# Two-tile router rows, and the third expert pair's weights loaded ahead of the first gather

## The chip, the core and the metric

The kernel runs on one core of one Trainium2 chip. The metric is the device time of one execution in microseconds; 2% decides a verdict, and the time before is the median of three runs.

## The reference

Two layers. Each has a token mixer (layer 0: RWKV-7, layer 1: stick-breaking attention), a 4-head cross-attention into 256 memory tokens, and a hierarchical mixture of experts (MoE). All are pre-RMSNorm with a residual add, on 512 tokens of 1024 channels in float32. The part that matters here:

```python
def _hierarchical_moe(h, wg, bg, we, be, w1, w3, w2):
    g_logits = (t @ wg) + bg                       # 4 groups
    group = jnp.argmax(g_logits, axis=-1)
    e_logits = ((t @ we) + be).reshape(-1, G, E)   # 8 experts in each group
    top_val, top_idx = lax.top_k(e_sel, TOP_K)     # two experts of the chosen group
    ...
    for gi in range(G):
        hid = silu(t @ w1) * (t @ w3)              # 1024 -> 256
        y = y + (hid * gate) @ w2                  # 256 -> 1024
```

## The kernel before, in words

All engines run hand-written queues and meet through semaphores. One big on-chip array (`arena`, cut into slots of 1024 columns by `at(slot, shape)`) and one more (`ring`) hold everything but the residual `h`.

In a layer the output projection of cross-attention (`xo0`, `xo1`, TensorE line L656) completes the residual tile by tile (4 tiles of 128 tokens), and the router runs between its groups. For each tile ScalarE (`moe_route_act`) squares the rows (L2317), scales and writes out the transposed tile that TensorE made (L562, into `xTE`), takes the root (L2323), scales the rows (L2306, into `tnE`) and stores them in DRAM (`normed_rows`, L2308). TensorE transposes (L552, through three banks, so the fourth transpose of a tile waits until ScalarE has written out the first), computes the logits (L2258) and ranks (L2275, L2276); VectorE chooses the experts. Then the MoE gathers rows from `normed_rows` by a table (GpSimd, L2601).

The 32 experts are worked as 16 pairs, n = 0 to 15. For a pair TensorE does the up matmuls (L2713), turns the hidden rows (L2728), turns the next pair's rows (L2698) and does the down matmuls of the pair before (L2738). A pair's weights are 4 pieces of up weights (`load_up`: w1 and w3 of two experts, L2544 and L2545) and 2 pieces of down weights (`load_down`, L2548), each 1 MB. Two buffer sets alternate, and pair 2's up weights have a place of their own (`w13x`, slots 12 to 20). SyncE issues all of these loads in one fixed order, and each waits until the pair before it in its buffer is done:

- `moe_first_loads`: pair 0, during cross-attention.
- `moe_route_loads`: the router's own weights; `moe_loads`: pair 1, as the ring's slots come free.
- Then, when all rows are stored, all logits done and the first gather has landed (`xg_in0`): pair 2's up weights into `w13x`.
- Up of pair 4 (after pair 0's up matmuls), up of pair 3 (after pair 1's up), down of pair 2 (after pair 0's down), down of pair 3 (after pair 1's down), up of pair 5 (after pair 3's up), and so on.

Slots 12 to 20 are `tnE` (4 tiles of rows, slots 12 to 16) and `xTE` (4 transposed tiles, slots 16 to 20) while the router runs, which is why pair 2's up weights wait for it. Slots 28 to 32 are the memory's keys and values, used in both layers.

Of the kernel before, what the change touches and what calls it, by code (L numbers as in the profile page):

```python
# [11 lines left out]
P = 128  # L12
C = 1024
T = 512
# [117 lines left out]
def trunk(nc, A, out, scratch):  # L132

    ctx = ExitStack()
    with ctx:
# [395 lines left out]
        def late_bank(name, n):  # L531

            return 5 + n % 3 if name[:3] == "ffn" else 4 + n % 4
# [20 lines left out]
        def late_evac(eng, name, t, dst, which, step=2):  # L554

            for k in range(which, KC, step):
                n = LATE0[name] + KC * t + k
                eng.wait_ge(S("late_turned"), n + 1)
                g = gainT[:, GAIN[name], k:k + 1]
                d, v = dst[:, k, P * t:P * t + P], PS[:, late_bank(name, n), 0:P]  # L560
                if which == 0 or step == 1:
                    eng.activation(d, v, ACT.Copy, scale=g).then_inc(S("late_act"), 1)  # L562
                else:
                    eng.tensor_scalar(d, v, g, None, ALU.mult).then_inc(S("late_vec"), 1)
# [1572 lines left out]
        def so_vec(vec):  # L2137
# [4 lines left out]


        NPE = NE // 2
        tnE = at(12, [NT, C])
        xTE = at(16, [KC, T])
        ringS = ring[:, :, :, :].rearrange("p r k n -> p (r k n)")


# [3 lines left out]
        w2e = [[split(arena[:, 6144 * a + 4096:6144 * a + 6144], [2, C]) for a in range(2)],  # L2153
               [split(ringS[:, 2048 * a:2048 * a + 2048], [2, C]) for a in range(2)]]
        w13x = [at(12 + 4 * a, [2, KC, F]) for a in range(2)]
        xg = [at(20 + p, [C]) for p in range(2)]
        xgT = [at(22 + p, [KC, P]) for p in range(2)]
        ye = [at(24 + p, [C]) for p in range(2)]
# [83 lines left out]

        def moe_route_loads(sp, l):

            sp.wait_ge(S("proj_filled"), FIRST[f"xo{l}"] + 1)
            sp.dma_start(wge[:, :, 0:G], A["moe_wg"][l].rearrange("(p k) n -> p k n", k=KC)).then_inc(S("route_in"), 16)
            sp.dma_start(wge[:, :, G:], A["moe_we"][l].rearrange("(p k) n -> p k n", k=KC)).then_inc(S("route_in"), 16)
            sp.dma_start(bge[:, 0:G], bcast(A["moe_bg"][l])).then_inc(S("route_in"), 16)
            sp.dma_start(bge[:, G:], bcast(A["moe_be"][l])).then_inc(S("route_in"), 16)

        def route_logits(pe, l, t):

            if t == 0:
                pe.wait_ge(S("route_in"), 64 * (l + 1))
            scores_read(pe, l, (0, 1, 3, 6)[t])
            for k in range(KC):
                tile_there(pe, f"ffn{l}", t, k)
                ins = pe.matmul(PS[:, 4, HD * t:HD * t + G + NE], xTE[:, k, P * t:P * t + P], wge[:, k, :],  # L2258
                                start=(k == 0), stop=(k == KC - 1))
            ins.then_inc(S("logits"), 1)  # L2260

# [39 lines left out]
        def moe_route_act(act, l):  # L2301
            name, ready = f"ffn{l}", h_tile_ready(f"xo{l}")

            def rows(t):
                act.wait_ge(S("ffn_rstd"), 5 * l + (1, 2, 4, 5)[t])
                act.activation(tnE[:, t, :], h[:, t, :], ACT.Copy, scale=rstd[:, t:t + 1]).then_inc(S("norm_rows"), 1)  # L2306
                act.wait_ge(S("norm_rows"), ROWS0[name] + t + 1)
                act.dma_start(scratch["rows"][P * t:P * t + P, :], tnE[:, t, :]).then_inc(S("rows_out"), 16)  # L2308

            act.activation(warm[:, :], gn_eps[:, :], ACT.Sqrt).then_inc(S("table_warm"), 1)  # L2310
            for t in range(NT):
                last = t == NT - 1
                ready(act, t)
                if last:
                    late_evac(act, name, t, xTE, 0, 1)
                end, total = 512 if last else C, sumsq[:, t:t + 1]
                act.activation(tnE[:, t, 0:end], h[:, t, 0:end], ACT.Square, accum_out=total).then_inc(S("ffn_norm"), 1)  # L2317
                if not last:
                    late_evac(act, name, t, xTE, 0, 1 if t else 2)
                act.wait_ge(S("ffn_norm"), 9 * l + (1, 3, 5, 8)[t])  # L2320
                if last:
                    act.wait_ge(S("ffn_rstd"), 5 * l + 3)
                act.activation(rms[:, t:t + 1], total, ACT.Sqrt, scale=1.0 / C,  # L2323
                               bias=half_mean[:, :] if last else ffn_eps[:, :]).then_inc(S("ffn_norm"), 1)
                if t and not last:
                    rows(t - 1)
                if t == NT - 2:
                    group_evacuated(act, FIRST[f"xo{l}"] + 12)
                    act.activation(tnE[:, NT - 1, 512:C], h[:, NT - 1, 512:C], ACT.Square, accum_out=half_sq[:, :])\
                        .then_inc(S("ffn_norm"), 1)  # L2330
                if t == NT - 2:
                    rows(t)
            rows(NT - 1)
            act.activation(warm[:, :], gn_eps[:, :], ACT.Exp).then_inc(S("table_warm"), 1)
            act.wait_ge(S("route_a"), 2 * l + 2)
            act.activation(gdiff, gdiff, ACT.Exp).then_inc(S("route_exp"), 1)
            act.activation(ed, ed, ACT.Exp).then_inc(S("route_exp"), 1)
# [223 lines left out]
        def moe_loads(sp, l):  # L2561


            assert UNITS.index(f"xo{l}") % RING == 2
            load_up(sp, l, 2, w13[1][0], S("w13_in1"))
            sp.wait_ge(S("proj_filled"), FIRST[f"xo{l}"] + 11)
            load_up(sp, l, 3, w13[1][1], S("w13_in1"))
            sp.wait_ge(S("proj_filled"), FIRST[f"xo{l}"] + 13)
            for a in range(2):
                load_down(sp, l, 2 + a, w2e[1][a], S("w2_in1"))  # L2570

            sp.wait_ge(S("rows_out"), 16 * NT * (l + 1))
            sp.wait_ge(S("logits"), NT * (l + 1))

            sp.wait_ge(S("xg_in0"), 16 * (NPE // 2 * l + 1))
            for a in range(2):
                load_up(sp, l, 4 + a, w13x[a], S("w13x_in"))

            def up_weights(n):
                sp.wait_ge(S("up_done"), NPE * l + (n - 3 if n == 4 else n - 1))  # L2580
                for a in range(2):
                    load_up(sp, l, 2 * n + a, w13[n % 2][a], S(f"w13_in{n % 2}"))

            def down_weights(n):

                sp.wait_ge(S("down_done"), NPE * l + n - 1)
                for a in range(2):
                    load_down(sp, l, 2 * n + a, w2e[n % 2][a], S(f"w2_in{n % 2}"))

            up_weights(4)  # L2590
            up_weights(3)
            down_weights(2)
            down_weights(3)
            for n in range(4, NPE):
                if n + 1 < NPE:
                    up_weights(n + 1)
                down_weights(n)
# [7 lines left out]
        def moe_pool(pool, l):  # L2605
# [6 lines left out]
            for p in range(2):  # L2612
                pool.memset(xg[p], 0.0).then_inc(S("xg_cleared"), 1)  # L2613
            pool.wait_ge(S("xg_cleared"), 2 * l + 2)
            pool.wait_ge(S("rows_out"), 16 * NT * (l + 1))
            pool.wait_ge(S("table_ready"), l + 1)
            for n in range(4):
                fetch(n)
# [112 lines left out]
        def hidT_out(act, rows):  # L2731
            return act.activation(hidT[:, :, 0:rows], bank(4, 4, P)[:, 0:2, 0:rows], ACT.Copy)

        def down(pe, p, n, half):
            for k in range(2):
                for a in range(n):
                    r = slice(BLK * a, BLK * a + BLK)
                    ins = pe.matmul(PS[r, 6 + half, :], hidT[:, k, r],  # L2738
                                    w2e[p][a][:, k, 512 * half:512 * half + 512], start=(k == 0), stop=(k == 1))
            return ins  # L2740

        def ye_free(eng, l, j, p):
# [11 lines left out]
        def moe_pe(pe, l):  # L2754
# [21 lines left out]
            def down_pair(n):  # L2776
                p = n % 2
                pe.wait_ge(S(f"w2_in{p}"), 32 * (NPE // 2 * l + n // 2 + 1))
                pe.wait_ge(S("hidT_ready"), NPE * l + n + 1)
                pe.wait_ge(S("ye_a"), NPE * l + n + l + 1)  # L2780
                down(pe, p, 2, 0).then_inc(S("down_half"), 1)
                pe.wait_ge(S("ye_v"), NPE * l + n + l + 1)
                down(pe, p, 2, 1).then_inc(S("down_done"), 1)

            pe.wait_ge(S("table_ready"), l + 1)
            for p in range(2):
# [131 lines left out]
        def further_pe(pe, l):  # L2918
# [6 lines left out]
            def body(j, at_step):  # L2925
                pe.wait_ge(S(f"over_gathered{l}"), 16 * (j + 1))
                step(at_step, 50)
                turn_rows(pe, 0, BLK).then_inc(st, 1)
                step(at_step, 52)
                up(pe, 0, 1, w13[0]).then_inc(st, 1)  # L2930
                step(at_step, 56)
                turn_hid(pe, BLK).then_inc(st, 1)
                step(at_step, 58)
                down(pe, 0, 1, 0)
                down(pe, 0, 1, 1).then_inc(st, 1)
                step(at_step, 61)
            further(pe, l, body)

# [203 lines left out]
```

## Time and profile before

| | |
|---|---|
| median of 3 runs | 1691.88 us (1688.39 to 1696.31) |
| profiled execution | 1693.46 us, span 1691.6 us |
| TensorE busy | 1527.1 us, 90% of the span |
| VectorE, ScalarE, GpSimd busy | 802.5, 418.7, 160.8 us |
| DMA | 315.04 MB, mean 186 GB/s |
| mean granted TensorE clock | 0.960 |

The span is from the first to the last instruction. The profile slices it in 40 parts; in the two MoE stretches (about 715 to 950 us and 1421 to 1650 us) the DMA engines are busy all the time, and moved 402 to 426 GB/s in a slice; in most slices between they are nearly idle. All times of day below are microseconds from the span's start.

### The profile page before, as it was taken

How to read it: one execution, taken by the hardware profiler on the slowest of the kernel's cores; microseconds unless marked ns; L12 is line 12 of the kernel's file. 1: busy time of each engine (PE TensorE's matmuls, PEld its weight loads, DVE VectorE, ACT ScalarE, POOL GpSimd, SP SyncE). 2: the span in 40 equal slices, each digit the busy share in tenths (PEclk: the TensorE clock that was granted, in tenths of full speed). 3: DMA queues.
4: the chain of work that ended last, by engine and by line, in shares of the span. 5: the costliest groups of instructions: out<-in, count | busy, mean ns of one | idle time of the engine just before them, and what ended most of it. 6: DMA issues, size and time to landing. Idle time of an engine off the chain costs nothing.

```text
span 1691.6 us, 28991 instructions
## 1 busy us (share of the span) xinstructions
PE 1527.1 (90%) x12509; PEld 943.0 (56%) x12509; DVE 802.5 (47%) x1403; ACT 418.7 (25%) x849; POOL 160.8 (10%) x183
## 2 busy tenths in 40 slices
PE   6999988989999999799788899999999997988777
PEld 4786777777645864534233388646468544333332
DVE  6655555653854355444121455546652544431225
ACT  2124255554201231301000120037321322100002
POOL 2000223230000000111110200000000001111101
PEclk9999999999999999799899999999999997989988
DMA  8208200011631412499999912220042116999995
GB/s 275 100 1 297 71 3 5 4 48 35 226 123 64 191 46 73 161 402 422 424 425 423 349 46 100 100 100 2 1 191 108 54 65 225 405 424 426 423 417 199
DMA packets 82338, 315.04 MB, mean 186 GB/s; under 512 B 17968, under 2 KB 19048, under 8 KB 57312
## 3 DMA queue, kind: packets, MB, share of 16 engines
q1 hardware_dynamic: 70112, 284.86, 43.3%
q0 software_dynamic: 10944, 24.10, 3.9%
q10 hardware_dynamic: 1152, 4.19, 0.6%
q8 instruction: 100, 1.64, 0.4%
q14 instruction: 30, 0.25, 0.0%
HBM read 306.86 MB, written 34.34 MB: 202 GB/s over the span
## 4 chain that ended last, share of the span: by engine, by line
PE 84%; issue 6%; DVE 5%; ACT 3%; DMA 1%; PEld 0%; SPq 0%; ACTq 0%; DVEq 0%; POOLq 0%
PE PS L789 20%; PE PS L2713 15%; PE PS L656 13%; PE PS L1441 9%; PE PS L2738 7%; PE PS L1834 2%; PE PS L1770 2%; PE PS L2698 2%; PE PS L2662 2%; PE PS L627 2%; PE PS L1810 1%; PE PS L2090 1%; PE PS L2111 1%; PE PS L552 1%; PE PS L2101 1%
## 5 line engine op out<-in xcount | busy, mean ns | idle before, releaser
L789 PE MATMUL PS<-arena,ring 128*128 128x256 f32 x1344 | 299.3, 383 | 2.9 <-DVE arena L933 2.9
L789 PEld LDWEIGHTS PS<-arena,ring 128*128 128x128 f32 x1344 | 255.6, 192 | 42.3 <-issue 6.4
L2713 PE MATMUL PS<-ring,arena 128*64 128x512 f32 x512 | 134.9, 687 | 54.4 <-issue 51.3
L656 PE MATMUL PS<-ring,arena 128*128 128x512 f32 x400 | 181.5, 600 | 0.7 <-ACT arena L2056 0.7
L2721 DVE TENSOR_TENSOR arena<-PS,arena 128x256 f32<-128x256 f32 x32 | 13.6, 424 | 253.3 <-PE PS L2728 235.0
L2713 PE MATMUL PS<-arena 128*64 128x512 f32 x512 | 116.3, 607 | 13.5 <-issue 10.7
L2713 PEld LDWEIGHTS PS<-ring,arena 128*64 128x64 f32 x512 | 44.2, 158 | 143.2 <-issue 139.5
L656 PEld LDWEIGHTS PS<-ring,arena 128*128 128x128 f32 x400 | 75.1, 193 | 83.3 <-issue 82.3
L2718 ACT ACTIVATE arena<-PS 128x256 f32<-128x256 f32 x32 | 12.3, 383 | 359.9 <-PE PS L2713 359.9
L838 DVE TENSOR_TENSOR arena<-arena,PS 128x512 f32<-128x512 f32 x56 | 36.8, 684 | 112.5 <-PE PS L789 112.4
L2713 PEld LDWEIGHTS PS<-arena 128*64 128x64 f32 x512 | 40.7, 140 | 87.4 <-issue 83.9
L1441 PE MATMUL PS<-ring 64*64 64x64 f32 (+1 forms) x3072 | 76.4, 237 | 8.3 <-issue 7.5
L831 ACT ACTIVATE arena<-PS 128x512 f32<-128x512 f32 x56 | 32.9, 595 | 204.2 <-PE PS L789 204.2
L1441 PEld LDWEIGHTS PS<-ring 64*64 64x64 f32 x3072 | 71.8, 136 | 17.3 <-issue 13.9
L1268 ACT ACTIVATE ring<-PS 128x512 f32<-128x512 f32 (+1 forms) x88 | 63.2, 752 | 64.1 <-PE PS L1441 60.2
L700 DVE TENSOR_TENSOR h<-h,PS 128x512 f32<-128x512 f32 x64 | 43.2, 685 | 75.2 <-PE PS L656 75.0
L1441 PE MATMUL PS<-arena 64*64 64x64 f32 (+1 forms) x2112 | 69.2, 244 | 9.3 <-issue 4.2
L687 DVE TENSOR_TENSOR arena<-arena 128x1024 f32<-128x1024 f32 x44 | 54.9, 1249 | 42.4 <-PE PS L789 36.6
L656 PE MATMUL PS<-arena 128*128 128x512 f32 x160 | 72.3, 595 | 0.0
L2613 POOL MEMSET arena<- 128x1024 f32 x4 | 3.7, 968 | 693.7 <-PE PS L656 693.7
L1441 PEld LDWEIGHTS PS<-arena 64*64 64x64 f32 x2112 | 58.6, 134 | 19.6 <-issue 7.4
L2738 PE MATMUL PS<-ring,arena 128*64 128x512 f32 x256 | 59.7, 609 | 1.0 <-issue 1.0
(336 smaller groups left out, 2248.6 us busy)
## 6 DMA issues: line engine op xcount, KB each, us to landing
arena<-in_moe_w SPq DMA_DIRECT2D x96, 1024.0 KB, 16.2
ring<-in_moe_w SPq DMA_DIRECT2D x96, 1024.0 KB, 14.3
ring<-in_sb_wqkv SPq DMA_DIRECT2D x6, 2048.0 KB, 9.4
ring<-in_xa_wq SPq DMA_DIRECT2D x4, 2048.0 KB, 8.6
ring<-in_xa_wo SPq DMA_DIRECT2D x4, 2048.0 KB, 14.2
ring<-in_xa_wkv SPq DMA_DIRECT2D x3, 2048.0 KB, 10.9
h<-in_x SPq DMA_DIRECT2D x8, 512.0 KB, 8.9
ring<-in_rw_wr SPq DMA_DIRECT2D x2, 2048.0 KB, 11.1
```

What stands on the lines that cost most here:

```text
L627: ins = pe.matmul(PS[:, BANK_OF[g], :], xt[:, k, P * t:P * t + P], ring[:, (u0 + half) % RING, k, :], start=(k == 0), stop=(k == KC - 1))
L656: ins = pe.matmul(PS[:, BANK_OF[g], :], rows(k), cols[:, k, :], start=(k == 0 and not grows), stop=(k == 3), skip_group_check=grows)
L687: vec.tensor_tensor(out, a, b, op).then_inc(S("quarters"), 1)
L700: ins = vec.tensor_tensor(v, v, group_out(vec, g), ALU.add)
L789: ins = pe.matmul(PS[:, BANK_OF[g], M * c:M * c + M], rows[:, k, o:o + P], cols[:, k, :], start=(c + k == 0 and not grows), stop=(k == 3), ...
L838: ins = vec.tensor_tensor(v, v, group_out(vec, FIRST[name] + n).rearrange("p (c n) -> p c n", c=2), ALU.add)
L1268: act.activation(dst, src, ACT.Copy).then_inc(S("pair_act_out"), 1)
L1441: return pe.matmul(out, lhs, rhs, start=start, stop=True, skip_group_check=True)
L1770: ins = pe.matmul(PS[:, BANK_OF[g], 0:M], rows[:, P * (j % 4):P * (j % 4) + P], mem_xT[:, k, :], start=(k == 0), stop=(k == KC - 1))
L1834: ins = pe.matmul(PS[:, BANK_OF[g], :], memV[:, m, XD * x + P * v:XD * x + P * v + P], probT[x % 2][:, m, :], start=(m == 0), stop=(m == 1))
L2713: ins = pe.matmul(bank(2, 2, F)[r, :, :], xgT[p][:, k, r], w[a][:, :, k, :], start=(k == 0), stop=(k == KC - 1))
L2738: ins = pe.matmul(PS[r, 6 + half, :], hidT[:, k, r], w2e[p][a][:, k, 512 * half:512 * half + 512], start=(k == 0), stop=(k == 1))
```

## The change: what it does

1. The router keeps two tiles in place of four: `tnE` is slots 12 to 14, `xTE` slots 14 to 16, and tile t uses place t % 2. So ScalarE now waits before it writes tile t over tile t - 2: tile 2's square waits for the store of tile 0's rows to have landed (`rows_out0`) and for logits 0; tile 3's transposed rows wait for logits 1, and its scaled rows for tile 1's store (`rows_out1`). Tile 3's squares go to a scratch (`wide_`).
2. Slots 16 to 20 are then free during the router: the up weights of expert 5 (half of pair 2) are loaded when the cross-attention's query projection is done. The up weights of expert 4 still wait for the router's stores and logits, but no longer for the first gather.
3. In layer 1 alone, pair 2's down weights go to slots 28 to 32 once the memory's values have been read for the last time, and leave their place in the later order.

ScalarE's queue in layer 0's router, from the scaled rows of tile 0 to the transposed tile 2. Before:

```order
L2306 ACTIVATE arena<-h,rstd 128x1024 [waits ffn_rstd]
L2308 DMA normed_rows<-arena 128x1024 [waits norm_rows]
L2317 ACTIVATE arena,sumsq<-h 128x1024 [waits proj_out_V]
L562 ACTIVATE arena<-PS,gainT 128x128 [waits late_turned] x8
L2323 ACTIVATE rms<-sumsq,ffn_eps 128x1 [waits ffn_norm]
```

and now:

```order
L2316 ACTIVATE arena<-h,rstd 128x1024 [waits ffn_rstd]
L2318 DMA normed_rows<-arena 128x1024 [waits norm_rows]
L2332 ACTIVATE arena,sumsq<-h 128x1024 [waits rows_out0,logits,proj_out_V]
L563 ACTIVATE arena<-PS,gainT 128x128 [waits late_turned] x8
L2339 ACTIVATE rms<-sumsq,ffn_eps 128x1 [waits ffn_norm]
```

Nothing is moved; the third instruction has two more waits, one of them on the DMA issued by the instruction right ahead of it.

SyncE's queue in layer 1, from pair 1's down weights to pair 5's up weights (w1 and w3 are up weights, w2 down weights). Before:

```order
L2548 DMA ring<-in_moe_w2 128x2048 [waits proj_filled]
L2548 DMA ring<-in_moe_w2 128x2048
L2544 DMA arena<-in_moe_w1 128x2048 [waits xg_in0,logits,rows_out]
L2545 DMA arena<-in_moe_w3 128x2048
L2544 DMA arena<-in_moe_w1 128x2048
L2545 DMA arena<-in_moe_w3 128x2048
L2544 DMA arena<-in_moe_w1 128x2048 [waits up_done]
...
L2548 DMA arena<-in_moe_w2 128x2048 [waits down_done]
L2548 DMA arena<-in_moe_w2 128x2048
L2548 DMA ring<-in_moe_w2 128x2048 [waits down_done]
L2548 DMA ring<-in_moe_w2 128x2048
L2544 DMA ring<-in_moe_w1 128x2048 [waits up_done]
```

and now:

```order
L2564 DMA ring<-in_moe_w2 128x2048 [waits proj_filled]
L2564 DMA ring<-in_moe_w2 128x2048
L2560 DMA arena<-in_moe_w1 128x2048 [waits logits,rows_out1,rows_out0]
L2561 DMA arena<-in_moe_w3 128x2048
L2560 DMA arena<-in_moe_w1 128x2048 [waits up_done]
...
L2564 DMA ring<-in_moe_w2 128x2048 [waits down_done]
L2564 DMA ring<-in_moe_w2 128x2048
L2560 DMA ring<-in_moe_w1 128x2048 [waits up_done]
```

Two pieces of up weights and both pieces of pair 2's down weights have left this part. In layer 1 they stand ahead of the router's weights instead:

```order
L2560 DMA arena<-in_moe_w1 128x2048 [waits proj_filled]
L2561 DMA arena<-in_moe_w3 128x2048
L2564 DMA arena<-in_moe_w2 128x2048 [waits proj_filled]
L2564 DMA arena<-in_moe_w2 128x2048
L2254 DMA arena<-in_moe_wg 128x8x4 [waits proj_filled]
```

In layer 0 the two up pieces move in the same way, and pair 2's down weights stay where they were. TensorE's, VectorE's and GpSimd's instructions keep their order.

```diff
@@ late_evac
-                d, v = dst[:, k, P * t:P * t + P], PS[:, late_bank(name, n), 0:P]
+                at_t = t % 2 if name[:3] == "ffn" else t
+                d, v = dst[:, k, P * at_t:P * at_t + P], PS[:, late_bank(name, n), 0:P]
@@ the places
-        tnE = at(12, [NT, C])
-        xTE = at(16, [KC, T])
+        tnE = at(12, [2, C])
+        xTE = at(14, [KC, 2 * P])
+        w2x = [at(28 + 2 * a, [2, C]) for a in range(2)]
@@ moe_route_loads
+            sp.wait_ge(S("proj_filled"), FIRST[f"xq{l}"] + 14)
+            load_up(sp, l, 5, w13x[1], S("w13x_in"))
+            if l == 1:
+                sp.wait_ge(S("proj_filled"), FIRST["xv1"] + 8)
+                for a in range(2):
+                    load_down(sp, l, 4 + a, w2x[a], S("w2_in0"))
@@ moe_route_act, rows(t)
+                if t == 3:
+                    act.wait_ge(S("rows_out1"), 16 * (2 * l + 1))
-                act.activation(tnE[:, t, :], h[:, t, :], ACT.Copy, scale=rstd[:, t:t + 1]).then_inc(S("norm_rows"), 1)
+                act.activation(tnE[:, t % 2, :], h[:, t, :], ACT.Copy, scale=rstd[:, t:t + 1]).then_inc(S("norm_rows"), 1)
-                act.dma_start(scratch["rows"][P * t:P * t + P, :], tnE[:, t, :]).then_inc(S("rows_out"), 16)
+                act.dma_start(scratch["rows"][P * t:P * t + P, :], tnE[:, t % 2, :])\
+                    .then_inc(S(f"rows_out{t % 2}"), 16)
@@ moe_route_act, the loop over tiles
+                if t >= 2:
+                    act.wait_ge(S("logits"), NT * l + t - 1)
                 if last:
                     late_evac(act, name, t, xTE, 0, 1)
+                if t == 2:
+                    act.wait_ge(S("rows_out0"), 16 * (2 * l + 1))
-                act.activation(tnE[:, t, 0:end], h[:, t, 0:end], ACT.Square, accum_out=total).then_inc(S("ffn_norm"), 1)
+                act.activation(wide_ if last else tnE[:, t % 2, :], h[:, t, 0:end], ACT.Square, accum_out=total)\
+                    .then_inc(S("ffn_norm"), 1)
@@ moe_loads
-            sp.wait_ge(S("xg_in0"), 16 * (NPE // 2 * l + 1))
-            for a in range(2):
-                load_up(sp, l, 4 + a, w13x[a], S("w13x_in"))
+            load_up(sp, l, 4, w13x[0], S("w13x_in"))
...
-            down_weights(2)
+            if l == 0:
+                down_weights(2)
@@ moe_pe, down_pair
+                w = w2x if l == 1 and n == 2 else w2e[p]
```

## Rows read from the trace of the kernel before

**Rows 1.** The page: the chain that ended last, shares by engine

```profile
PE 84%; issue 6%; DVE 5%; ACT 3%; DMA 1%; PEld 0%; SPq 0%; ACTq 0%; DVEq 0%; POOLq 0%
```

**Rows 2.** TensorE's waits, 715 to 960 us: us in total, times, longest

```profile
PE PS L2713 <- issue: 31.1, 10, 5.5
```

**Rows 3.** TensorE's waits, 1415 to 1680 us

```profile
PE PS L2713 <- issue: 31.0, 11, 5.8
```

**Rows 4.** Stretches: busy by engine, granted clock, DMA share, GB/s

```profile
728.00:729.00 1.00, 0.23 (x3) 0.03 (x1) 0.97 (x3) 0.00 (x0) 0.00 (x1) 1.00 0.76 147
729.00:753.60 24.60, 23.85 (x118) 9.35 (x120) 11.81 (x32) 2.73 (x6) 4.20 (x4) 1.00 1.00 407
1434.00:1435.00 1.00, 0.41 (x4) 0.21 (x2) 0.96 (x3) 0.00 (x0) 0.00 (x0) 1.00 0.58 147
1435.00:1461.00 26.00, 24.09 (x118) 9.26 (x120) 13.17 (x35) 2.73 (x6) 4.24 (x4) 1.00 1.00 401
1469.00:1470.00 1.00, 1.00 (x7) 0.42 (x8) 1.00 (x3) 0.00 (x0) 0.14 (x1) 1.00 0.74 246
1500.00:1640.00 140.00, 113.75 (x512) 44.81 (x511) 32.14 (x68) 11.44 (x26) 16.18 (x16) 0.91 1.01 423
```

**Rows 5.** ScalarE and its queue in order of time, layer 0: start, us

```profile
680.37 0.35 ACTq L2308 DMA_DIRECT2D normed_rows<-arena  x1
680.76 1.06 ACT L2317 ACTIVATE arena<-h 128x1024 f32<-128x1024 f32 x1 [0.43 <-ACT arena L2306]
```

**Rows 6.** Store of tile rows: KB, us from issue to landing, 675 to 690 us, then all 8 stores

```profile
normed_rows<-arena ACTq DMA_DIRECT2D x1, 512.0 KB, 2.6
...
normed_rows<-arena ACTq DMA_DIRECT2D x8, 512.0 KB, 4.1
```

**Rows 7.** TensorE in order of time, layer 0's router

```profile
682.22 0.38 PE L552 MATMUL PS<-ident,h 128*128 128x128 f32 x1 [1.60 <-ACT arena L562]
682.43 2.09 PE L2258 MATMUL PS<-arena 128*128 128x36 f32 x16
684.33 2.05 PE L656 MATMUL PS<-ring,arena 128*128 128x512 f32 x2
695.72 0.60 PE L552 MATMUL PS<-ident,h 128*128 128x128 f32 x3 [1.46 <-DVE h L700]
```

**Rows 8.** VectorE in order of time, layer 0's router

```profile
684.63 0.25 DVE L2369 SCALAR_TENSOR_TENSOR arena<-PS,rstd,arena 128x36 f32<-128x36 f32 x1 [5.13 <-PE PS L2258]
```

**Rows 9.** ScalarE and its queue, layer 1

```profile
1386.36 0.33 ACTq L2308 DMA_DIRECT2D normed_rows<-arena  x1
1386.73 1.06 ACT L2317 ACTIVATE arena<-h 128x1024 f32<-128x1024 f32 x1 [0.40 <-ACT arena L2306]
```

**Rows 10.** SyncE's queue in order of time, both layers: start, us

```profile
715.37 0.33 SPq L2544 DMA_DIRECT2D arena<-in_moe_w  x1
...
727.19 0.33 SPq L2544 DMA_DIRECT2D arena<-in_moe_w  x1
...
1433.37 0.33 SPq L2544 DMA_DIRECT2D arena<-in_moe_w  x1
...
1459.73 0.80 SPq L2548 DMA_DIRECT2D ring<-in_moe_w  x2
1467.80 0.33 SPq L2544 DMA_DIRECT2D ring<-in_moe_w  x1
```

**Rows 11.** DMA of the gathers and row stores, 1435 to 1461 us: packets, MB, share

```profile
q0 software_dynamic: 432, 0.73, 7.6%
```

**Rows 12.** The chain that ended last, in order of time: before pair 3 of layer 1

```profile
1459.69 0.98 issue
```

**Rows 13.** TensorE in order of time, layer 0: pair 3's up matmuls

```profile
753.36 7.04 PE L2713 MATMUL PS<-ring,arena 128*64 128x512 f32 x32
```

**Rows 14.** A stretch of the router, and one of cross-attention ahead of it

```profile
684.00:687.40 3.40, 3.40 (x8) 1.80 (x8) 2.39 (x12) 0.62 (x2) 0.00 (x0) 0.51 0.00 0
610.00:634.00 24.00, 22.23 (x85) 13.85 (x84) 13.07 (x27) 9.97 (x24) 0.00 (x0) 1.00 0.00 1
```

More of the change, by code:

```diff
@@ L2257, in route_logits @@
                 tile_there(pe, f"ffn{l}", t, k)
-                ins = pe.matmul(PS[:, 4, HD * t:HD * t + G + NE], xTE[:, k, P * t:P * t + P], wge[:, k, :],
+                ins = pe.matmul(PS[:, 4, HD * t:HD * t + G + NE], xTE[:, k, P * (t % 2):P * (t % 2) + P], wge[:, k, :],
                                 start=(k == 0), stop=(k == KC - 1))
@@ L2328, in moe_route_act @@
                     group_evacuated(act, FIRST[f"xo{l}"] + 12)
-                    act.activation(tnE[:, NT - 1, 512:C], h[:, NT - 1, 512:C], ACT.Square, accum_out=half_sq[:, :])\
+                    act.activation(wide_, h[:, NT - 1, 512:C], ACT.Square, accum_out=half_sq[:, :])\
                         .then_inc(S("ffn_norm"), 1)
@@ L2570, in moe_loads @@
                 load_down(sp, l, 2 + a, w2e[1][a], S("w2_in1"))
-            sp.wait_ge(S("rows_out"), 16 * NT * (l + 1))
+            for t in range(2):
+                sp.wait_ge(S(f"rows_out{t}"), 32 * (l + 1))
             sp.wait_ge(S("logits"), NT * (l + 1))
-            sp.wait_ge(S("xg_in0"), 16 * (NPE // 2 * l + 1))
-            for a in range(2):
-                load_up(sp, l, 4 + a, w13x[a], S("w13x_in"))
+            load_up(sp, l, 4, w13x[0], S("w13x_in"))
             def up_weights(n):
@@ L2614, in moe_pool @@
             pool.wait_ge(S("xg_cleared"), 2 * l + 2)
-            pool.wait_ge(S("rows_out"), 16 * NT * (l + 1))
+            for t in range(2):
+                pool.wait_ge(S(f"rows_out{t}"), 32 * (l + 1))
             pool.wait_ge(S("table_ready"), l + 1)
@@ L2732, in hidT_out, with down @@
             return act.activation(hidT[:, :, 0:rows], bank(4, 4, P)[:, 0:2, 0:rows], ACT.Copy)
-        def down(pe, p, n, half):
+        def down(pe, w, n, half):
             for k in range(2):
@@ L2738, in down @@
                     ins = pe.matmul(PS[r, 6 + half, :], hidT[:, k, r],
-                                    w2e[p][a][:, k, 512 * half:512 * half + 512], start=(k == 0), stop=(k == 1))
+                                    w[a][:, k, 512 * half:512 * half + 512], start=(k == 0), stop=(k == 1))
             return ins
@@ L2780, in down_pair @@
                 pe.wait_ge(S("ye_a"), NPE * l + n + l + 1)
-                down(pe, p, 2, 0).then_inc(S("down_half"), 1)
+                w = w2x if l == 1 and n == 2 else w2e[p]
+                down(pe, w, 2, 0).then_inc(S("down_half"), 1)
                 pe.wait_ge(S("ye_v"), NPE * l + n + l + 1)
-                down(pe, p, 2, 1).then_inc(S("down_done"), 1)
+                down(pe, w, 2, 1).then_inc(S("down_done"), 1)
             pe.wait_ge(S("table_ready"), l + 1)
@@ L2933, in body @@
                 step(at_step, 58)
-                down(pe, 0, 1, 0)
-                down(pe, 0, 1, 1).then_inc(st, 1)
+                down(pe, w2e[0], 1, 0)
+                down(pe, w2e[0], 1, 1).then_inc(st, 1)
                 step(at_step, 61)
```

## The prediction

> **What bounds the kernel now.** I read the page first. TensorE makes up 84% of the chain that ended last; "issue", time in which TensorE waits for something that the profile doesn't name, is the second largest share of that chain [rows 1]. So I asked for TensorE's waits in the two MoE stretches. There the waits on "issue" ahead of the up matmuls sum to 31.1 us in layer 0 and 31.0 us in layer 1 [rows 2, 3]. The view of stretches says what they are: from pair 3 or so the DMA engines are busy 100% of the time at some 401 to 423 GB/s [rows 4]. Those waits are weights that haven't arrived. The MoE is therefore bound by the weight stream, which starts to matter once it runs without a gap, and the time at which it last had a gap is the number to look for. The router ahead of it is another case: hardly any DMA, and a tight exchange between TensorE, ScalarE and VectorE, in which each waits for the others. There a late ScalarE is a late everything.
>
> So the change has two sides: bytes taken out of the stream (good only as far as the stream can start the rest earlier), and two waits put into the router (bad unless something else is later).
>
> **Part 1: the router's new wait.** In layer 0 ScalarE issues the store of tile 0's rows at 680.37 and starts tile 2's square at 680.76 [rows 5]. The changed kernel's square waits for that store to land. It takes 2.6 us from issue to landing there [rows 6], so the square starts at 680.37 + 2.6 = 682.97, which is 2.2 us late. Layer 1 has the same picture, 1386.36 and 1386.73 [rows 9]: 1386.36 + 2.6 - 1386.73 = 2.2 us. Queued behind the square on ScalarE are the eight write-outs of the transposed tile 2. TensorE's fourth transpose of tile 2 already waited 1.60 us for the first of them, until 682.22, and it heads TensorE's queue: behind it are the logits of tile 1 at 682.43 and the next projection matmuls [rows 7]. So TensorE is late by the full 2.2 us. VectorE had waited 5.13 us for exactly these logits and begins its choice of experts at 684.63 [rows 8], so it is late by 2.2 us too, and the later waits of this part (TensorE's 1.46 us for VectorE at 695.72 [rows 7]) move along. I find nothing that absorbs the delay before the table and the first gather, which the last choices feed. Cost: 2 x 2.2 = **+4.4 us**.
>
> What bounds it: the lowest landing is the 2.6 us used; the median over the eight stores is 4.1 us [rows 6], which would give 680.37 + 4.1 - 680.76 = 3.7 us per layer, 7.4 in all. I keep 2.2, since the row is of the very store. A wait can't come out below nothing here, for TensorE was already waiting for this chain.
>
> [...]
>
> The other new waits cost nothing: logits 0 ended well before tile 2, and logits 1, even 2.2 us late, end about 687 (682.43 + 2.09 + 2.2), long before tile 3's transposes at 695.72 [rows 7]. If these were late after all, tile 3 would move by their lateness only.
>
> **Part 2: the loads moved ahead.** Expert 5's up weights are 2 pieces of 1.05 MB, 5.0 us at 423 GB/s [rows 4]; in layer 1 pair 2's down weights are the same again. They now run in cross-attention, where the DMA engines moved 1 GB/s [rows 14]. Free. In layer 1 they also stand ahead of the router's weights and pair 1's first up pieces on SyncE; those are needed some 30 us later, so 5 us in the queue do no harm.
>
> **Part 3: what the stream gains in layer 0.** Before, `w13x` (4 pieces) is issued at 715.37 and pair 4's up weights at 727.19, when pair 0's matmuls end [rows 10]. Between 728 and 729 the rate falls to 147 GB/s, and from 729 on the engines are full [rows 4]. So `w13x` ran out just as pair 4's weights began: the rest of the stream starts when TensorE releases a buffer, not when bytes before it are through. Taking 2.1 MB out ahead of that point only widens the gap. The most it can give is the part of that 1 us in which engines were still finishing `w13x`, and more on the slowest of the 16 engines, because a semaphore needs all of them. By bytes, pair 3's weights end after 8.4 MB plus some 0.65 MB of gathers at 407 GB/s, 22.3 us after 729, at 751.3; TensorE had to wait for none of them at 753.36 [rows 13]. So the slowest engine is at most 2.1 us behind. I take 0.7 us, between 0 and 2.1, near the mean engine. Dropping the wait for the first gather moves a load that ends long before it is used: 0.
>
> **Part 4: the same in layer 1, plus the down weights.** The first part is as in layer 0: pair 4's up weights at 1433.37 [rows 10], rate 147 GB/s at 1434, full from 1435 [rows 4]. Then the queue before holds 10 pieces (10.49 MB) and 0.73 MB of gathers and row stores [rows 11] until pair 3's down weights can start: 11.2 MB / 401 GB/s = 28.0 us, at 1463.0. Without pair 2's down weights it is 9.1 MB, 22.8 us, at 1457.8. But pair 3's down weights are issued only at 1459.73, when pair 1's down matmuls end [rows 10], and a first packet follows some 1.5 us behind its issue (1433.37 to the refill near 1435), so they start at 1461.2. Of 5.2 us, 1.8 are left. The next load is pair 5's, issued at 1467.80 [rows 10], first packets about 1469.3; before, the rate had already dropped to 246 GB/s at 1469 [rows 4], that is, on most engines this load was released late even then. What can still move it is TensorE's own wait of 0.98 us at 1459.69 [rows 12] for pair 3's up weights, which may go when `w13x` is shorter, and the slowest engine: by bytes pair 3's weights end at 1435 + 9.0/0.401 = 1457.4, but TensorE got them at 1459.69 + 0.98 = 1460.7 [rows 12], so that engine is 3.3 us behind and would catch up in the new gaps. So between 0 and 3.3 us; I take **2.0**, of which 1.0 is the wait. After pair 5 the backlog grows (TensorE waits again and again), no load is released late, and the gain stays to the end.
>
> **The sum**: +4.4 - 0.7 - 2.0 = +1.7 us. On the profiled execution's 1693.46 us (span 1691.6) this is 1695.2. That execution lies 1.6 us above the median of 1691.88, so the median comes to **1693.6 us**. A measurement of this kernel can't tell under 0.5% (8.5 us) from no change, so this is "the same". By the bounds the sum goes from 4.4 - 5.4 = -1.0 to 7.4 (with no gain), and the clock below adds up to 3.4: 1690.9 to 1702.7.
>
> **Rivals.**
>
> A, slower: the wait also costs clock. TensorE's idle 1.60 us at 680.6 becomes 3.8 us. After the present one the granted clock is 0.51 from 684.0 to 687.4 [rows 14], the 1.2 GHz level, and the two projection matmuls at 684.33 take 2.05 us [rows 7], about double. A second stretch of that length would cost 1.7 us per layer. With the store landing in 4.1 us rather than 2.6: 7.4 + 3.4 - 1.0 = +9.8, 1701.7 us. It decides from a landing of about 4 us together with a second fall of the clock. For it: the median landing. Against: both stores of tile 0 are the quick ones, and the stretch that would be slow is full of small matmuls that mind the clock less. The Trainium skill, TensorE: Matmul & The Clock Gate, "HAM oscillation", tells of kernels whose matmuls wait for DMAs and fall to the half clock again and again; the trace agrees that the clock falls after TensorE's pauses, and only a run shows whether once or twice here.
>
> B, faster: the stream counts in full. If its end is set by the bytes since 715.37 and 1421, it ends 2.1 MB earlier in layer 0 and 4.2 MB in layer 1: 5.0 + 9.9 = 14.9 us, less 4.4: -10.5, 1681.4 us. For it: the stretch from 1500 to 1640 is full to 1.01 [rows 4]. Against: the two seconds at 147 GB/s, and the issue times of rows 10, which the change doesn't move.
>
> C, hidden: the new wait costs nothing (the store lands earlier than I read, or TensorE finds other work), and the gain stays: -2.7, 1689.2 us. Against: TensorE's queue has a fixed order and its head is what waits.
>
> **Chances.** Forecast 0.66, A 0.12, B 0.12, C 0.10. Of these only B is over 0.5% faster and A slower: faster 0.12, same 0.76, slower 0.12. The forecast's own range is 1690.9 to 1700; three runs before spread by 8 us, so with C and the near parts of A and of half gains toward B the range is 1686 to 1701.
>
> **What would show it.** ScalarE's tile 2 square starts about 2.6 us after the issue of tile 0's store, in both layers, and TensorE's wait ahead of the fourth transpose is near 3.8 us instead of 1.60. From there to the first gather everything is 2.2 us later, or more with a second stretch at the low clock. SyncE issues expert 5's weights in cross-attention with no wait growing there. The DMA is idle for some microseconds ahead of pair 4's up weights, and in layer 1 again ahead of pair 3's down and perhaps pair 5's up weights. The "issue" waits of layer 0 stay at 30 to 31 us, those of layer 1 fall by about 2. I am wrong if layer 1's fall by 8 or more (B), or if the transpose's wait doesn't grow (C).

## The result, and the profile after

The changed kernel is slower, by less than 2%: median 1698.83 us against 1691.80 us of the kernel before in 20 runs each (1691.38 to 1702.39, 1688.09 to 1700.86). The ratio is 1.0034 with a 95% interval of 1.0023 to 1.0044, or 5.7 us (3.9 to 7.4) on 1692. The forecast was 1693.6 us, "the same", in a range of 1686 to 1701. The profiled execution took 1697.87 us; its span is 1696.0 us, 4.4 us more than before.

The page's chain has hardly moved; TensorE still makes up 84% of it [rows 1]:

```profile
span 1696.0 us, 28995 instructions
PE 84%; issue 6%; DVE 6%; ACT 3%; DMA 1%; PEld 0%; SPq 0%; DVEq 0%; ACTq 0%; POOLq 0%
```

**The router's wait.** ScalarE and its queue in order of time (start, us, what, and in brackets what it waited for), layer 0 and then layer 1 [rows 5, 9]:

```profile
678.88 0.35 ACTq L2318 DMA_DIRECT2D normed_rows<-arena  x1
681.58 1.06 ACT L2332 ACTIVATE arena<-h 128x1024 f32<-128x1024 f32 x1 [2.73 <-DMA normed_rows<-arena]
...
1389.59 0.33 ACTq L2318 DMA_DIRECT2D normed_rows<-arena  x1
1392.63 1.06 ACT L2332 ACTIVATE arena<-h 128x1024 f32<-128x1024 f32 x1 [3.08 <-DMA normed_rows<-arena]
```

The square starts 2.70 and 3.04 us after the store's issue, where it started 0.39 and 0.37 us after it before: 2.3 and 2.7 us late. TensorE's fourth transpose of tile 2 shows the same, and what stands behind it in its queue shows more [rows 7]:

```profile
683.03 0.38 PE L552 MATMUL PS<-ident,h 128*128 128x128 f32 x1 [3.90 <-ACT arena L563]
683.24 2.81 PE L2266 MATMUL PS<-arena 128*128 128x36 f32 x16
685.86 2.05 PE L657 MATMUL PS<-ring,arena 128*128 128x512 f32 x2
688.13 1.92 PE L657 MATMUL PS<-ring,arena 128*128 128x512 f32 x2
698.17 0.60 PE L552 MATMUL PS<-ident,h 128*128 128x128 f32 x3 [1.46 <-DVE h L701]
...
1394.09 0.48 PE L552 MATMUL PS<-ident,h 128*128 128x128 f32 x1 [4.25 <-ACT arena L563]
1394.36 3.47 PE L2266 MATMUL PS<-arena 128*128 128x36 f32 x16
```

The logits of tile 1 take 2.81 and 3.47 us, where they took 2.09 and 1.87, and two pairs of projection matmuls are slow, not one. From the fourth transpose to tile 3's transposes it is 698.17 - 683.03 = 15.1 us, where it was 695.72 - 682.22 = 13.5 us. The view of stretches (busy time by engine, then the granted clock, DMA share and GB/s) says why; the second row is layer 1's:

```profile
683.50:690.30 6.80, 6.80 (x24) 4.52 (x24) 3.55 (x18) 0.94 (x4) 0.00 (x0) 0.53 0.01 2
1393.60:1400.30 6.70, 6.21 (x22) 5.02 (x23) 2.05 (x10) 1.68 (x8) 0.00 (x0) 0.53 0.00 0
```

The clock stays at its low level (1.2 of 2.4 GHz) for some 6.8 us behind TensorE's pause, twice the 3.4 us of before [rows 14]. That is rival A's second slow stretch. The matmuls in it are small, and the prediction had held that small ones mind the clock less. They don't: a tile's logits take 3.47 us when they lie wholly at the low clock and 1.87 us at the full one, nearly double.

**The stream.** SyncE's queue [rows 10] and the rates [rows 4] around pair 4's and pair 3's loads, layer 1. The four loads listed are expert 4's up weights, pair 4's up weights, pair 3's down and pair 5's up weights:

```profile
1417.32 0.33 SPq L2560 DMA_DIRECT2D arena<-in_moe_w  x1
...
1442.41 0.33 SPq L2560 DMA_DIRECT2D arena<-in_moe_w  x1
...
1468.77 0.89 SPq L2564 DMA_DIRECT2D ring<-in_moe_w  x2
1475.64 0.33 SPq L2560 DMA_DIRECT2D ring<-in_moe_w  x1
```

```profile
1440.00:1443.00 3.00, 3.00 (x18) 1.27 (x15) 0.17 (x1) 0.38 (x1) 0.00 (x0) 1.00 0.00 0
1443.00:1444.00 1.00, 0.44 (x5) 0.25 (x3) 0.96 (x3) 0.00 (x0) 0.00 (x0) 1.00 0.75 131
1445.00:1466.00 21.00, 21.00 (x106) 8.29 (x108) 10.54 (x29) 2.13 (x5) 2.50 (x4) 1.00 1.01 407
1466.00:1471.00 5.00, 5.00 (x26) 1.74 (x24) 2.46 (x10) 0.60 (x1) 1.59 (x2) 1.00 0.51 152
1500.00:1640.00 140.00, 113.82 (x518) 45.00 (x516) 34.16 (x71) 12.30 (x27) 17.19 (x17) 0.91 1.01 424
```

Both gaps are there: nothing moves ahead of pair 4's up weights, and between 1466 and 1471 the engines are half idle, ahead of pair 3's down weights. After that the stream is as full as before (424 GB/s against 423). TensorE's waits for weights, layer 0 and layer 1 [rows 2, 3] (us in total, times, longest):

```profile
PE PS L2730 <- issue: 29.7, 10, 5.5
...
PE PS L2730 <- issue: 30.0, 10, 5.8
```

Layer 0's were forecast to stay at 30 to 31 us and layer 1's to fall by about 2. They fell by 1.4 and 1.0 us; a fall of 8 or more, the sign of rival B, isn't there.

**A measure for both sides.** Two intervals between rows of TensorE's order of time separate the router from the stream. A runs from the third transpose of tile 2 (the last work ahead of the new wait) to the start of pair 1's up matmuls. B runs from there to the start of pair 15's. Their ends for the changed kernel are, in layer 0, 678.86, 732.46 and 941.93, and in layer 1:

```profile
1389.56 0.27 PE L552 MATMUL PS<-ident,h 128*128 128x128 f32 x1
...
1444.96 7.09 PE L2730 MATMUL PS<-ring,arena 128*64 128x512 f32 x32 [1.52 <-DVE arena L2720]
...
1653.43 8.72 PE L2730 MATMUL PS<-ring,arena 128*64 128x512 f32 x32 [3.79 <-issue]
```

| us | A, layer 0 | A, layer 1 | B, layer 0 | B, layer 1 |
|---|---|---|---|---|
| before | 49.4 | 49.6 | 209.4 | 212.1 |
| changed | 53.6 | 55.4 | 209.5 | 208.5 |
| difference | +4.2 | +5.8 | +0.1 | -3.7 |

The sum is +6.4 us. The spans differ by only 4.4, so what lies outside the intervals was 2.0 us shorter in the changed kernel's profile. One profile each can't say how much of -3.7 is the change's; the experiments' profiles say more.

### The profile page after: what moved, and what is told of

Same layout as the page of the kernel before. It is cut to its first block, busy times and chain, and to the rows that moved or that the text cites. A ratio compares the mean times of both kernels' runs of the same rounds, so it can differ in the third digit from the quotient of the medians.

```text
span 1696.0 us, 28995 instructions
## 1 busy us (share of the span) xinstructions
PE 1528.5 (90%) x12509; PEld 945.3 (56%) x12509; DVE 802.7 (47%) x1403; ACT 418.8 (25%) x849; POOL 160.8 (9%) x183
## 4 chain that ended last, share of the span: by engine, by line
PE 84%; issue 6%; DVE 6%; ACT 3%; DMA 1%; PEld 0%; SPq 0%; DVEq 0%; ACTq 0%; POOLq 0%
PE PS L790 20%; PE PS L2730 15%; PE PS L657 13%; PE PS L1442 9%; PE PS L2755 7%; PE PS L1835 2%; PE PS L1771 2%; PE PS L2715 2%; PE PS L628 2%; PE PS L1811 1%; PE PS L2679 1%; PE PS L2091 1%; PE PS L2112 1%; PE PS L2102 1%; PE PS L2266 1%
## 5 line engine op out<-in xcount | busy, mean ns | idle before, releaser
L2738 DVE TENSOR_TENSOR arena<-PS,arena 128x256 f32<-128x256 f32 x32 | 13.6, 424 | 250.6 <-PE PS L2745 230.3
L1442 PEld LDWEIGHTS PS<-ring 64*64 64x64 f32 x3072 | 70.7, 134 | 15.1 <-issue 11.6
```

Source lines behind the costliest of these rows:

```text
L1442: return pe.matmul(out, lhs, rhs, start=start, stop=True, skip_group_check=True)
```

## The experiments

Ratios are against the kernel before, run on the same chip, with the 95% interval. The intervals reach about 0.15% (2.6 us) to either side, so the ratios tell 8 us from 0 and hardly 2 us from 0. A and B of each profile carry the finer readings, but they scatter as well: the same kernel profiled twice ("no stall", below) has an A of 50.5 and 52.1 us in layer 0 and a B of 210.0 and 208.6 us in layer 1. A single difference under 2 us is no finding.

### The wait alone

```diff
@@ the kernel before, moe_route_act
+                if t == 2:
+                    act.wait_ge(S("rows_out"), 16 * (NT * l + 1))
```

> The kernel before with one thing added: tile 2's square waits for tile 0's row store, as in the changed kernel, though it overwrites nothing. Theory (the wait and the clock stretch behind it cost, about 2.3 to 2.7 us of stall and 1.2 to 3.1 us of clock a layer): 7 to 10 us slower, the transpose's wait near 3.9 us, a second slow stretch of the clock behind it. Rival (the wait alone is hidden or costs only its 4.4 us; the rest of the change's cost is in the moved loads): 0 to 5 us slower.

Measured: 1.0045 (1.0029 to 1.0062), 7.6 us slower. A is 54.1 and 53.8 us. The fourth transpose's wait and the stretch behind it:

```profile
683.47 0.38 PE L552 MATMUL PS<-ident,h 128*128 128x128 f32 x1 [4.55 <-ACT arena L562]
683.68 3.38 PE L2258 MATMUL PS<-arena 128*128 128x36 f32 x16
```

```profile
683.40:690.20 6.80, 6.73 (x23) 5.08 (x24) 2.62 (x13) 1.47 (x6) 0.00 (x0) 0.53 0.00 0
```

One wait, on a place that nothing needs, brings the whole loss, its doubled slow stretch included. The rival, 0 to 5 us with no further cost, only touches the low end of the interval (0.29%, 4.9 us), and the trace shows the clock's stretch that it left out.

### The router alone

The changed kernel with all expert loads, their waits and pair 2's down place as before.

```diff
@@ the changed kernel, moe_route_loads and moe_loads
-            sp.wait_ge(S("proj_filled"), FIRST[f"xq{l}"] + 14)
-            load_up(sp, l, 5, w13x[1], S("w13x_in"))
...
-            load_up(sp, l, 4, w13x[0], S("w13x_in"))
+            sp.wait_ge(S("xg_in0"), 16 * (NPE // 2 * l + 1))
+            for a in range(2):
+                load_up(sp, l, 4 + a, w13x[a], S("w13x_in"))
```

> The changed kernel's whole router with two tiles, but all expert loads where they were before, the wait for the first gather included. Theory (the router is all loss, and nothing but the store's wait in it costs): as the one with the wait alone, 7 to 10 us slower than before, within 1 us of it; against the changed kernel 3 to 4 us slower, which is what the moved loads give. Rival (the moved loads give nothing, or the logits' waits cost too): equal to the changed kernel, or slower than the wait alone.

Measured: 1.0055 (1.0030 to 1.0079), 9.3 us slower; A is 53.8 and 53.4 us. It lies beside the wait alone (0.10% or 1.7 us apart, where within 1 us was forecast; inside both intervals), with the same A to 0.4 us. So the logits' waits and the wait for tile 1's store cost nothing that can be seen. Against the changed kernel it is 0.21% (3.6 us) slower, as forecast, but the intervals overlap (this one begins at 1.0030, the changed kernel's ends at 1.0044), so the ratios don't show that the moved loads give anything.

### The wait filled with matmuls

```diff
@@ the changed kernel, cross_pe, tile 2's transposes
+                        for _ in range(20):
+                            pe.matmul(PS[:, 4, 416:512], ident[:, :], ident[:, 0:96], start=True, stop=True)
```

> The changed kernel with 20 small matmuls (96 columns, their result unused) put into TensorE's wait ahead of the fourth transpose of tile 2, where it waits 3.9 to 4.3 us anyway. Theory (TensorE's pause costs clock): no or one short slow stretch behind it, logits 1 back to about 1.9 us; 1 to 4 us faster than the changed kernel, 3 to 5 us slower than before. Rival (the slow stretches come from elsewhere): as the changed kernel, 5 to 6 us slower than before.

Measured: 1.0018 (1.0001 to 1.0035), 3.0 us slower than before. TensorE in order of time (the view has two entries for each of these matmuls, so x40 is the 20), and the stretch that was slow:

```profile
679.12 0.27 PE L552 MATMUL PS<-ident,h 128*128 128x128 f32 x1
679.23 4.60 PE L1847 MATMUL PS<-ident 128*128 128x96 f32 x40
683.80 0.35 PE L552 MATMUL PS<-ident,h 128*128 128x128 f32 x1
683.98 1.89 PE L2272 MATMUL PS<-arena 128*128 128x36 f32 x16
```

```profile
684.50:691.00 6.50, 6.20 (x33) 3.94 (x32) 4.36 (x22) 2.52 (x7) 0.00 (x0) 1.00 0.30 96
```

The store is waited for as before (2.70 to 3.34 us and 2.66 to 3.04 us from its issue to the square, over layers 0 and 1 of the four kernels with the wait), and the filling is even about half a microsecond too long in layer 0 (4.68 us from third to fourth transpose, where it was 4.17; 4.55 and 4.53 in layer 1), yet the clock stays at its full level and the logits are back at 1.89 us. A is 52.4 and 53.7 us, 1.2 and 1.7 us less than in the changed kernel. From the fourth transpose to tile 3's it is 13.6 and 13.5 us again. So TensorE's pause is what brings the slow stretch. Of A's +4.2 and +5.8 us the stall is 2.3 and 2.7; 13.5 us of work behind it became 15.1 and 15.0, which is 1.6 and 1.5 of clock. What is left (0.3 and 1.6) lies in the later low stretch around the table and pair 0, whose up matmuls took 9.17 and 10.05 us against 8.46 and 8.83. That part varies from profile to profile: this filled kernel has 8.42 and 10.04.

A longer pause isn't needed for the long stretch, though. It also follows the old pause of 1.6 us at times. This is layer 0 of a kernel without the stall ("gather wait back", below), whose clock is at 0.50 from 682 to 688.5 us:

```profile
680.90 0.38 PE L552 MATMUL PS<-ident,h 128*128 128x128 f32 x1 [1.66 <-ACT arena L563]
681.12 2.73 PE L2266 MATMUL PS<-arena 128*128 128x36 f32 x16
696.05 0.60 PE L552 MATMUL PS<-ident,h 128*128 128x128 f32 x3 [1.46 <-DVE h L701]
```

That is 15.1 us from the fourth transpose to tile 3's. Nine profiles here (the kernel before's, and eight of kernels with neither the new wait there nor a filling) have the old pause unfilled, 18 layers in all: in 12 the low stretch is about 3.4 us long, in 2 there is none, and in 4 it is about 6.8 us. Behind the grown pause it is 6.8 us in 6 of 6 layers, and in the 4 layers with a filled pause there is none. So the grown pause makes certain what the old one brought in 4 of 18. Averaged over these profiles it adds about 1.2 us a layer, not the 1.6 and 1.5 by which the changed kernel's profile exceeds that of the kernel before, which has two of the shorter ones.

### No stall: tile 2's square over place 1

Place 1 holds only tile 1's discarded squares at that time, so the wait moves down to tile 2's scaled rows.

```diff
@@ the changed kernel, moe_route_act
-                if t == 2:
-                    act.wait_ge(S("rows_out0"), 16 * (2 * l + 1))
-                act.activation(wide_ if last else tnE[:, t % 2, :], h[:, t, 0:end], ACT.Square, accum_out=total)\
+                act.activation(wide_ if last else tnE[:, min(t, 1), :], h[:, t, 0:end], ACT.Square, accum_out=total)\
@@ rows(t)
-                if t == 3:
-                    act.wait_ge(S("rows_out1"), 16 * (2 * l + 1))
+                if t >= 2:
+                    act.wait_ge(S(f"rows_out{t % 2}"), 16 * (2 * l + 1))
```

> The changed kernel, but tile 2's square is written over place 1 of the rows (where only tile 1's discarded squares stand), so that the wait for tile 0's store moves down to tile 2's scaled rows, some 10 us later. Theory: no stall, the transpose's wait back to 1.6 us, layer 1's stream gain stays: 3 to 5 us faster than before (0.2 to 0.3%). Rival (gain was luck of the clock, or depends on the late start): no faster than before.

> The kernel without the stall (tile 2's square elsewhere), both loads early, once more, since its first comparison left -0.10% with an interval over zero. Theory: 2 to 4 us faster than before. Rival: nothing.

Measured: 0.9990 (0.9973 to 1.0006) and, the second time, 0.9977 (0.9965 to 0.9989): 1.7 and 3.9 us faster. The wait is gone from ScalarE and back to its old size on TensorE:

```profile
676.97 0.35 ACTq L2318 DMA_DIRECT2D normed_rows<-arena  x1
677.42 1.06 ACT L2330 ACTIVATE arena<-h 128x1024 f32<-128x1024 f32 x1 [0.48 <-ACT arena L2316]
```

```profile
678.87 0.38 PE L552 MATMUL PS<-ident,h 128*128 128x128 f32 x1 [1.66 <-ACT arena L563]
679.09 1.87 PE L2266 MATMUL PS<-arena 128*128 128x36 f32 x16
```

A is 50.5 and 49.9 us in the first profile, 52.1 and 49.8 us in the second. Everything else of the change is still in. This version beats the changed kernel clearly, and the kernel before in its second set of runs; in the first the interval reaches to no difference, and 1.7 us is less than the 3 to 5 forecast.

### Which early load gives the gain

Three kernels without the stall: without the early down weights (twice), without the early up weights (both halves are loaded behind the first gather, as in the kernel before), and with expert 4's load waiting for the first gather again.

```diff
@@ no early down weights
-            if l == 1:
-                sp.wait_ge(S("proj_filled"), FIRST["xv1"] + 8)
-                for a in range(2):
-                    load_down(sp, l, 4 + a, w2x[a], S("w2_in0"))
...
@@ no early up weights
-            sp.wait_ge(S("proj_filled"), FIRST[f"xq{l}"] + 14)
-            load_up(sp, l, 5, w13x[1], S("w13x_in"))
...
-            load_up(sp, l, 4, w13x[0], S("w13x_in"))
+            sp.wait_ge(S("xg_in0"), 16 * (NPE // 2 * l + 1))
+            for a in range(2):
+                load_up(sp, l, 4 + a, w13x[a], S("w13x_in"))
@@ gather wait back
+            sp.wait_ge(S("xg_in0"), 16 * (NPE // 2 * l + 1))
             load_up(sp, l, 4, w13x[0], S("w13x_in"))
```

> The kernel without the stall (tile 2's square elsewhere), and layer 1's down weights of pair 2 back in their place in the stream; only expert 5's up weights are early. Theory (releases bind: the down weights open the gap ahead of pair 3's down weights): 2 to 3 us slower than the one with both, so 0.5 to 2 us faster than before. Rival (most comes from the shorter load ahead of pair 4): as the one with both.

> The kernel without the stall and without the early down weights, once more beside the one with them. Theory now (after its first run: layer 1's early down weights only open a gap and give nothing): within 1 us of the one with both, pair 1 to pair 15 in about 209.5 us in both layers. Rival (down weights worth 2 us): 2 us slower.

> The kernel without the stall, pair 2's up weights all loaded after the first gather as before; only layer 1's down weights of pair 2 are early. Theory (taking bytes out ahead of pair 4's release gives next to nothing): within 1 us of the one with both, 2 to 4 us faster than before. Rival (the slowest DMA engine is carried over from that load): 2 us slower than the one with both.

> The kernel without the stall, with the wait of expert 4's up weights for the first gather put back. Theory (that load ends long before its use): no difference to the same kernel without the wait, within 0.7 us. Rival (the dropped wait frees the stream earlier): 2 us slower or more.

Measured, with B of layers 0 and 1 in us:

| | ratio | B |
|---|---|---|
| both early (no stall) | 0.9990, 0.9977 | 209.4, 210.0; 209.4, 208.6 |
| no early down | 0.9983 (0.9970 to 0.9996), 0.9988 (0.9972 to 1.0003) | 209.6, 209.7; 209.4, 209.9 |
| no early up | 0.9983 (0.9968 to 0.9999) | 209.8, 211.4 |
| gather wait back | 0.9975 (0.9964 to 0.9987) | 209.4, 210.0 |

The ratios can't be told apart. B hints at one thing: the kernel without the early up weights has 211.4 in layer 1, near the 212.1 of before, with a wait for pair 3's weights, which is 0.98 us in the kernel before [rows 12]. Chain in order of time, no early up weights:

```profile
1461.71 0.50 issue
1462.21 7.09 PE PS L2728 x32
```

So on B the two forecasts came out the wrong way round: leaving out the up weights was to change nothing and has the worst B, leaving out the down weights was to cost 2 to 3 us and its ratios are no worse (its second run was forecast after the first, and held). Over all profiles, TensorE waits for pair 3's weights in 5 of the 8 layers in which all up weights are loaded behind the gather (0.17 to 0.98 us), and in 2 of the 20 others. But the kernel with the wait alone, which loads as before, doesn't wait there in either layer and has a B of 209.7 in layer 1, like the kernels with early loads. The gain is there on average, not every time. Dropping the gather's wait does nothing, as forecast.

### The small pause filled

The kernel without the stall, with 8 of the unused matmuls in the 1.6 us wait.

> The kernel without the stall, with 8 small matmuls (their result unused) in the 1.6 us that TensorE waits ahead of the fourth transpose even so. Theory (a pause of TensorE is what brings the slow stretch at 684 us): the stretch goes, 1 to 3 us faster than without them. Rival (the pause is too short to matter): no difference.

Measured: 0.9981 (0.9966 to 0.9997), 1.5 us less than the first ratio of the unfilled kernel and 0.7 us more than the second. There is no low stretch behind the pause in either layer; but the unfilled kernel had none in layer 0 of its first profile either. A (51.1 and 50.8 us) isn't better: pair 0's up matmuls, in the later low stretch, took 9.82 and 9.32 us here. A miss, or too small for this.

### The kernel before, with the load moved in time only

Its router is untouched. Once pair 2's four up pieces don't wait for the gather; once half of them don't.

```diff
@@ the kernel before, moe_loads: no gather wait
-            sp.wait_ge(S("xg_in0"), 16 * (NPE // 2 * l + 1))
@@ the kernel before, moe_loads: split
+            load_up(sp, l, 4, w13x[0], S("w13x_in"))
             sp.wait_ge(S("xg_in0"), 16 * (NPE // 2 * l + 1))
-            for a in range(2):
-                load_up(sp, l, 4 + a, w13x[a], S("w13x_in"))
+            load_up(sp, l, 5, w13x[1], S("w13x_in"))
```

> The kernel before with one wait taken out: pair 2's up weights (4 pieces, still behind the router's stores and logits) don't wait for the first gather. Theory (what the early up weights give is that the 16 DMA engines are all through before pair 4's weights are released, so that the slowest starts level): the load is done before pair 0's matmuls end, no wait for pair 3's up weights, pair 1 to pair 15 in about 209.4 us in both layers; but its last pieces collide with the first gather, which lands up to 2 us later: 0 to 2 us faster than before. Rival (fewer bytes are what counts): no faster than before.

> The kernel before with half of pair 2's up weights ahead of the wait for the first gather and half behind it. Theory (as above, the slowest engine levelled) : the gather undisturbed (TensorE waits 4.5 us for it as before), pair 1 to pair 15 in about 209.4 us: 1 to 3 us faster than before, without any change of the router. Rival (fewer bytes in the stream are what counts): as before.

Measured: 1.0003 (0.9988 to 1.0019) without the wait, 0.9983 (0.9965 to 1.0001) split. Neither can be told from the kernel before, nor from the other. B is 209.4 and 210.2 us, and 209.6 and 209.5 us. Without the wait the first gather comes late:

```profile
714.75 1.97 PE L2697 MATMUL PS<-ident,arena 128*128 128x128 f32 x8 [5.81 <-DMA arena<-normed_rows,table]
```

TensorE's wait for it is 5.81 us in layer 0 and 6.39 in layer 1, where it was 4.49 and 4.63 before, so with 4 MB of loads ahead of it the gather is waited for 1.3 and 1.8 us longer. Split, the wait is 4.43 and 4.74 us. A is 51.8 and 52.2 us without the wait, but also 51.4 and 51.1 split, so the gather is only a part of that; in both kernels pair 0's up matmuls took 9.5 to 10.0 us against 8.46 and 8.83.

No byte has left this part of the stream in these two kernels, and layer 1's B is 210.2 and 209.5, not 212.1. That fits the thought behind them, that the load has to be through on all 16 engines before pair 4's weights are released, and not that bytes have to leave. It doesn't show it: the wait alone, with its loads as before, had 209.7 as well.

## Why the prediction was right, and where not

The time lay in its range and the class was right, but the likeliest value was 1693.6 and the kernel takes about 1.692 x 3.4 = 5.7 us more than before, not 1.7.

- **The stall** (+4.4): right in place and mechanism, 2.3 + 2.7 = 5.0 us. The store landed as its row said in layer 0 (2.6 us) and later in layer 1 (2.9 us); the median of 4.1 us didn't come, in this kernel or in the three others with the wait. The prediction's "hardly any DMA" in the router was misread: pair 1's weights still moved at 434 GB/s between 676 and 677 us of the kernel before. They were through when tile 0's store was issued (0 GB/s from 680 to 681), so the stall's price didn't suffer.
- **The clock** (0 in the sum; 1.7 us a layer in rival A): this is the term that was mis-sized. Behind the pause of 3.9 and 4.3 us the slow stretch was doubled in both layers of the changed kernel, of the wait alone and of the router alone. Against the profile of before it cost 1.6 and 1.5 us, and filling the pause took it away; against the average of the profiles with the old pause it cost about 1.2 us a layer. I had taken rival A as a whole, tied to a store of 4.1 us. The clock's half of it needed only the pause itself, which the sum already had. The reason against it, that the small matmuls there mind the clock less, was wrong (3.47 us against 1.87).
- **The gain of layer 0** (0.7): 0.3 at most. The four profiles with the up weights late have a B of 209.3 to 210.5 (mean 209.8), the ten with them early, or moved in time, 209.3 to 209.6 (mean 209.4). One profile of the four, the router alone with 210.5, makes most of the difference.
- **The gain of layer 1** (2.0): about 1.8, loosely. B is 211.0 in the mean of three with all late, 209.8 in the mean of four with the up weights early or moved in time, 209.2 in the mean of six with the down weights early too. The up part is 1.2 and the down part 0.6, where the working had hung on both gaps alike. Each is smaller than the scatter of its profiles: the three late ones go from 209.7 to 212.1, and the six with both early lie at 208.4 to 208.6 or at 210.0 to 210.1, the same kernel once in either group. The one profile with the down weights alone early has 211.4, no gain at all, so the 0.6 isn't shown. That the total came near 2.0 is in part luck. The profile of before is the worst of the late ones, so its difference of 3.7 us to the changed kernel's is no measure of the change. That it is the slowest DMA engine that is levelled is argued, not shown: no view shows single engines.
- **Rivals.** B (15 us of bytes) is out: both gaps opened, and the waits for weights fell by 1.4 and 1.0 us. C is out: nothing covered the wait. The sum as measured: 5.0 of stall + 3.1 of clock behind it - 0.3 - 1.8 = 6.0 us, or 5.3 us with the clock's average of 2.4, against 5.7 (3.9 to 7.4) in the runs. The gains don't carry this: the loss is the stall and the clock.

## What to carry to other kernels

When a buffer is made smaller, ask of each write what it overwrites: here all that had to wait for the store was the write of a discarded result, and sending that to a place already free took the whole loss back. Before counting bytes taken out of a saturated stream as time, look whether a release, and not the bytes before it, starts what comes next: here 15 us of bytes gave about 2. And price a new stall on TensorE as the pause plus a longer slow stretch behind it, if the trace already shows a slow stretch behind a shorter pause in the same place; look at several profiles first, for that stretch can differ from one execution to the next.

## What the runs showed of the hardware that was not expected

- Matmuls whose result nobody uses, put into a 3.9 us pause, kept the granted clock at 1.00 where it had been 0.53 for 6.8 us, and took 1.2 and 1.7 us off A although in layer 0 they overran the wait by 0.5 us.
- The same 1.6 us pause in the same place was followed by no low stretch, by one of about 3.4 us or by one of about 6.8 us (2, 12 and 4 of 18 layers), the last two in one and the same execution.
- Two stores of the same size and place in the program, in one execution, landed in 2.6 and 2.9 us; in the other kernels with the wait the longer one (up to 3.34 us to the square) was layer 0's.
- The kernel before had medians of 1691.8, 1696.7, 1694.2 and 1692.8 us in the four sets of runs (three of them on chips 2, 11 and 3), a spread nearly as large as the whole effect. So only ratios inside a set can be compared, and intervals inside one trace where several profiles agree.
